# A decoder step on one core: tile 7's values ahead of two output parts, other places for identity matmuls and counts, V's sets in another order

## What is computed

```
z = rmsnorm(x, norm1_g) @ w_in            # rq rk rv rg mq mk mv
ret_o, state = retention_chunked(rq, rk, rv, state_ret)
moba_o = moba_attend_seq(mq, k_past + mk, v_past + mv)
mix = concat(groupnorm(ret_o) * ret_norm_g * silu(rg), moba_o)
h = x + mix @ w_out
n = rmsnorm(h, norm2_g)
logits = n @ router_w + router_b
top_v, top_i = top_k(logits, 4)
gates = softmax(top_v) spread over the experts top_i
for e in 32 experts:                      # 2048 gate/up columns, d_ff = 1024
    acc += gates[:, e] * (swiglu(n @ w_gate_up[e] + b_gate_up[e]) @ w_down[e] + b_down[e])
y = rmsnorm(h + acc, final_norm_g)
```

## Time and profile before

| what | value |
|---|---|
| time, median of 3 runs | 1268.71 us (1266.96 to 1270.87) |
| profiled execution, its own time | 1270.82 us |
| its span, first to last instruction | 1269.0 us |
| PE busy | 1207.8 us (95%) |
| DVE, ACT, POOL busy | 384.2, 232.7, 120.3 us |
| bytes moved | 500.64 MB, mean 395 GB/s |
| mean granted TensorE clock | 0.983 of full speed |
| chain that ended last | PE 61%, DMA 26%, DVE 7% |

### The profile page before, as it was taken

The page is one execution under the profiler, slowest core; times in us unless marked ns, Lnnn a source line. Parts: engine busy times, 40 slices in busy tenths (PEclk is TensorE's granted clock), DMA queues, the critical chain, the costliest instruction groups (busy, mean ns, idle before and its releaser), DMA issues.

```text
span 1269.0 us, 17410 instructions
## 1 busy us (share of the span) xinstructions
PE 1207.8 (95%) x7256; PEld 517.4 (41%) x7256; DVE 384.2 (30%) x552; ACT 232.7 (18%) x529; POOL 120.3 (9%) x117
## 2 busy tenths in 40 slices
PE   6999998699999999999999999999999999999997
PEld 3455445345534434343433434343434434343432
DVE  4999964153411211111122111111112211111113
ACT  3021153024201121110112112010102121111103
POOL 2222446641000000000000000000000000000000
PEclk8999999889899999999999999999999999999999
DMA  8999889968799999999999999999999999999994
GB/s 334 378 363 357 314 297 326 387 243 319 280 415 430 428 429 429 428 429 429 429 427 429 429 428 429 429 429 427 429 429 428 430 428 429 428 428 428 427 428 199
DMA packets 56604, 500.64 MB, mean 395 GB/s; under 512 B 6393, under 2 KB 6801, under 8 KB 27761
## 3 DMA queue, kind: packets, MB, share of 16 engines
q1 hardware_dynamic: 42128, 430.55, 81.1%
q0 software_dynamic: 14432, 69.47, 14.7%
HBM read 495.29 MB, written 4.72 MB: 394 GB/s over the span
## 4 chain that ended last, share of the span: by engine, by line
PE 61%; DMA 26%; DVE 7%; issue 4%; ACT 1%; SPq 0%; POOL 0%; DVEq 0%; POOLq 0%; ACTq 0%
PE psum L940 22%; DMA arena<-w_gate_up 21%; PE psum L971 12%; PE psum L852 6%; DVE arena L1430 5%; DMA arena<-w_down 3%; PE psum L858 2%; PE psum L502 2%; PE psum L697 2%; PE psum L870 2%; PE psum L589 2%; PE psum L882 2%; DMA arena<-cache_k,arena 1%; PE psum L889 1%; PE psum L428 1%
## 5 line engine op out<-in xcount | busy, mean ns | idle before, releaser
L940 PE MATMUL psum<-arena 128*64 128x512 f32 x1920 | 422.7, 594 | 15.7 <-DMA arena<-w_gate_up 15.6
L940 PEld LDWEIGHTS psum<-arena 128*64 128x64 f32 x1920 | 134.8, 137 | 300.1 <-issue 265.0
L1758 DVE TENSOR_SCALAR arena<-psum 128x512 f32<-128x512 f32 x32 | 22.1, 692 | 682.8 <-PE psum L940 643.5
L971 PE MATMUL psum<-arena 128*64 128x512 f32 x960 | 212.6, 595 | 0.0
L1096 ACT ACTIVATE arena<-psum 64x512 f32<-64x512 f32 (+3 forms) x184 | 93.5, 509 | 370.2 <-PE psum L971 170.7
L1430 DVE STREAM_TRANSPOSE arena<-arena 128x2048 f32<-128x2048 f32 x32 | 121.4, 3920 | 3.1 <-PE psum L488 1.9
L971 PEld LDWEIGHTS psum<-arena 128*64 128x64 f32 x960 | 66.4, 137 | 124.2 <-issue 122.4
L502 PE MATMUL psum<-arena 128*128 128x512 f32 x224 | 107.1, 617 | 0.5 <-ACT arena L1096 0.4
L1313 ACT ACTIVATE arena<-arena 128x512 f32<-128x512 f32 x30 | 18.9, 631 | 419.4 <-DVE arena L1758 419.4
L1096 ACT ACTIVATE arena<-psum,arena 128x128 f32<-128x128 f32 (+2 forms) x182 | 53.6, 397 | 171.2 <-PE psum L502 115.8
L852 PE MATMUL psum<-arena 128*128 128x128 f32 x512 | 80.1, 302 | 0.4 <-DVE arena L1679 0.4
(11 more groups left out here) (242 smaller groups left out, 724.3 us busy)
## 6 DMA issues: line engine op xcount, KB each, us to landing
arena<-w_gate_up SPq DMA_DIRECT2D x128, 2048.0 KB, 29.7
arena<-w_down SPq DMA_DIRECT2D x63, 2048.0 KB, 32.9
arena<-w_in SPq DMA_DIRECT2D x7, 2048.0 KB, 18.3
arena<-w_out SPq DMA_DIRECT2D x2, 2048.0 KB, 13.9
out<-arena SPq DMA_DIRECT2D x4, 512.0 KB, 3.0
out<-arena POOLq DMA_DIRECT2D x1, 2048.0 KB, 12.5
arena<-w_down SPq DMA_DIRECT2D x2, 1024.0 KB, 34.0
arena<-x_prompt SPq DMA_DIRECT2D x2, 512.0 KB, 5.6
```

What stands on the lines that cost most here:

```text
L940: last = mm(psum[64 * g:64 * (g + 1), b, :], xt[:, 2 * kk + m, lhs], gate_slot[slot][:, m, c:c + 512], start=False, stop=kk == 3 and m == ...
L971: last = mm(psum[64 * g:64 * (g + 1), 2, :], at_sb[:, m, SLOTS * q:SLOTS * (q + 1)], down_slot[slot][:, m, 512 * g:512 * (g + 1)], start=q ...
```

## The change

Eight edits, in the order of the diff. TensorE's `p_transposes(7)` and `values(7)` stand ahead of two output parts and of `sample_state(2)` and `(3)`, instead of behind them, and `evacuate_pt(7)` on ScalarE stands ahead of the sigmoid of the retention gate. `norm_transposes(1)` stands ahead of tile 0's logits, with two identity matmuls ahead of it; the identity matmul that stood ahead of tile 1's logits stands behind them; one more stands between the two groups of counts. The counts per pair stand behind the counts of ranks instead of behind the gather, and write bank 0 instead of bank 5. GpSimd's set 14 stands ahead of `v_block(1)`.

```
@@ tensor
             retention_output(0)
             retention_output(1)
+            pt = p_transposes(7)
+            values(7, pt)
             pe.wait_ge(own_ready, 1)
             output_part(1, 0, 5, attention)
             sample_state(2)
...
             output_part(0, 1, 6, attention)
             sample_state(3)
-            pt = p_transposes(7)
-            values(7, pt)
...
+            stay_awake(4, 2)
+            pe.wait_ge(hn_ready, 3)
+            norm_transposes(1)
             pe.wait_ge(a_empty, n_0[0])
             pe.wait_ge(d_empty, n_0[1])
             pe.wait_ge(router_in, 32)
             logits(0)
-            pe.wait_ge(hn_ready, 3)
-            norm_transposes(1)
             pe.wait_ge(a_empty, n_2)
             logits(2).then_inc(lg_full, 1)
-            stay_awake(7, 1)
             pe.wait_ge(a_empty, A.n)
             pe.wait_ge(d_empty, V.n)
             logits(1).then_inc(lg_full, 1)
+            stay_awake(7, 1)
...
             count(2, earlier, 2, start=False, stop=False)
+            stay_awake(7, 1)
             pe.wait_ge(picked_ready, 3)
             count(1, earlier, 1, start=False, stop=True)
             count(2, ones, 1, start=False, stop=True).then_inc(rank_full, 1)
+            for tile in range(TILES):
+                last = mm(psum[:, 0, 0:E], ones, picked[:, tile, :], start=tile == 0, stop=tile == TILES - 1)
+            last.then_inc(rank_full, 1)
...
             gather(0, 1)
-            for tile in range(TILES):
-                last = count(3, ones, tile, start=tile == 0, stop=tile == TILES - 1)
-            last.then_inc(rank_full, 1)
@@ scalar
             evacuate(ret_o[:, 1].rearrange("p h d -> p (h d)"))
+            evacuate_pt(7)
             wait_all(act, mark["z6"])
...
-            evacuate_pt(7)
@@ vector
-            tot = psum[:, 5, 3 * E:4 * E].rearrange("p (n e) -> p n e", e=2)
+            tot = psum[:, 0, 0:E].rearrange("p (n e) -> p n e", e=2)
@@ gpsimd
             v_set(13)
+            v_set(14)
             v_block(1)
-            v_set(14)
             v_set(15)
```

## The result

| | before | after |
|---|---|---|
| median, 20 runs each | 1268.12 us (1265.17 to 1272.44) | 1271.18 us (1266.64 to 1277.43) |
| ratio, 95% interval | | 1.0028 (1.0016 to 1.0041) |
| profiled execution, span | 1270.82, 1269.0 us | 1272.72, 1270.9 us |

The changed kernel takes 3.1 us more, by about the bound of 0.3%. I had forecast 1267.2, with 1270.9 as the upper end: the median lies 0.3 us above the range, and on the other side of no change.

A forecast was written before the change was run, and what follows sets the result against it. Bound by the expert-weight stream, so the loop start sets the end: +1.8 - 1.6 - 1.4 - 2.3 = -3.5 us on the profiled 1270.8 gives 1267.3, rounded with small change to 1267.2 us; range 1264.2 to 1270.9.

The forecast's parts named there:

- What bounds the kernel: Expert loop: bound by the weight stream; an earlier loop start moves the end one for one, until 6.6 us of pause are used.
- Part 1: Tile 7's transposes and `values(7)` ahead of two output parts: VectorE's states come later, costing +1.8 us on both paths.
- Part 2: Last V sets earlier: set 15 lands at 272.7 to 275.9, median 273.2, so no wait; far end costs 1.6 us.
- a landing after 274.3: Sign of being wrong: set 15 landing later than 274.3 us, when `values(7)` needs it halfway.
- Rival (b): GpSimd's `v_block(3)` multiply holds up VectorE's long product, +1.3 us on both paths: 1268.5 us; chance 0.20.
- part 3: Tile 1's transposes ahead of the logits, with identity matmuls: gather starts 1.6 us earlier (-2.1 + 0.35 + 0.1).
- Part 4: Pairs counted ahead of the gather: loop starts 2.45 us behind the gather instead of 3.9, a gain of 1.4 us.
- the gather's clock: Gather ahead of the loop: ran 10.4 us near 1.2 GHz, 6.4 at full clock; bounds 0 and -4.0, taken as -2.3 us.

The follow-up runs named there:

- e12: e7 with a buffer of its own for `v_block(3)`, so GpSimd makes it right behind `v_block(2)`; ratio 1.0009 to the kernel before.
- e7: Changed kernel with `load_turn(0)`, the 2 MB first expert load, held until set 14 has been used; ratio 1.0002 to the kernel before.
- e2: Kernel before with only tile 7's transposes and values moved ahead and set 14 ahead of `v_block(1)`, router part as before; 1274.78 us, ratio 1.0047.
- e4: Changed kernel with GpSimd's memset of y and `y_zero` ahead of the store of the states; 1273.75 us, ratio 1.0031 to the kernel before.
- e9: Changed kernel unaltered, run again as the control on the second chip; ratio 1.0018 to the kernel before.
- e10: e7 and e3 joined: first expert load held, and VectorE's states of head 2 behind the norm's last product; ratio 0.9992 to the kernel before.
- e1: Changed kernel with tile 7's transposes, values and ScalarE copy put back in their old places; 1265.84 us, ratio 0.9975 to the kernel before.
- e3: Changed kernel with VectorE's `new_states(2)` behind the last long product of the norm; 1269.79 us, ratio 0.9998 to the kernel before.
- e8: Kernel before with only GpSimd's set 14 moved ahead of `v_block(1)`; ratio 1.0017 to the kernel before.

## Where the prediction was right and where it failed

**What bounds the kernel** held. The span followed the start of the loop in every experiment, and the pause at the loop start took up most of the stream's later start: 5.0 of 6.6 us.

**Part 1, the order of the work: right.** I reckoned +1.8 us from moving `values(7)`; e12, in which TensorE doesn't wait for set 15 and VectorE's product isn't blocked, measured +1.72.

**Part 2: the step that failed.** "I take the median, 273.2, as most sets are at it: no wait." The set landed at about 276.2, beyond even the bound of 275.9, and the second half waited 3.51 us for it; the prediction had itself named a landing after 274.3 as a sign of being wrong. Two terms were too small, the landing and, further down, the issue.

The landing first. The row mixed sets of two kinds, and the trace of before could have told them apart. The same view of line 1904 there, first for the gathers issued from 240 to 258 us, then for the last four:

```profile
L1904 POOL DMA_INDIRECT arena<-cache_v,arena x9: 999/1003/1058, 240.3 to 258.0; - x9
...
DMA to landing us min/median/max: 8.3/8.4/9.3
```

```profile
L1904 POOL DMA_INDIRECT arena<-cache_v,arena x4: 1003/1003/1004, 263.3 to 267.2; - x4
...
DMA to landing us min/median/max: 11.0/11.1/11.5
```

The long landings were not a tail of all sets: they were all four of set 15, whose first gather was issued at 263.28, right behind `load_turn(0)`:

```profile
263.02 0.35 SPq L2008 DMA_DIRECT2D arena<-w_gate_up  x1
```

Before, no one waited for them. The question to ask of the set was whether its transfer shares the DMA, and the answer, 11.0 to 11.5 us behind 264.4, would have been a wait of 1.1 to 1.6 us as the likeliest case. e7 shows the cause.

The landing explains 2.9 of the 3.51 us (11.7 instead of 8.8). The issue explains more than the rest: I had the last gather 6.6 us ahead of the mark (271.01 - 264.4), and it was issued 4.93 us ahead of it (269.36 - 264.43), 1.7 us too late against a margin of 1.1. Even at the median landing TensorE would have waited 0.5 us. I had let set 15 start 2.6 us behind the start of `values(6)` (260.5 - 257.93). After, GpSimd's `v_block(1)` lay in between (the rows at 258.37 and 260.44), and it was 4.2 us; in e2 nothing but `values(6)` held the set, and it was 4.1 all the same (261.48 - 257.39). So the half of `values(6)` with the handing over to GpSimd took 1.5 us more than I gave it.

The bound was short for a third reason, because it priced the wait alone. Behind a wait of 3.51 us TensorE's clock was down, and the second half took 3.56 + 1.95 - 3.67 = 1.84 us more than before. Of all terms this was in none. It is no fixed price either: in e4 and e9 nothing was lost behind the wait.

**Rival (b) happened, and was priced right**: +1.3 us by my reckoning, 2.95 - 1.75 = 1.20 measured, and 1.20 in e12 against e7. All five profiled executions with the product behind that multiply show 2.95. I gave it 0.20 since the rows before showed only GpSimd paying. The rule of the Trainium skill that stood beside it ("SBUF — State Buffer", "Who interferes with whom": whoever of the two comes first blocks the other) agrees with every meeting here, those in which VectorE came second (2.95, 3.07 us) as well as those in which GpSimd did (2.54 in the earlier trace rows, 2.95 in e10).

The store's delay after the mark adds up: 1.72 (order) + 3.51 (wait) + 1.84 (clock) + 1.20 (product) = 8.27; measured 25.72 - 17.46 = 8.26. I had forecast the first term alone. On the other path, to the projection, VectorE's 8.26 met 1.0 us of slack (its product ended at 286.13 before, and the transposes began at 287.12), and the transposes behind the 1.96 us wait took 3.11 us to the output part instead of 1.89: 8.26 - 1.0 + 1.2 = 8.5, measured 26.55 - 18.00 = 8.55.

**Parts 3 and 4 and the gather: the sum was right, two terms of it were not.** From the end of the projection to the loop I reckoned -5.3 us; measured 25.13 - 30.32 = -5.2. But part 3 brought +0.1 instead of -1.6. The logits were done sooner (TensorE's counts, behind a wait of 0.93 us for VectorE, begin at 328.26, 11.01 us behind the projection, where before it was 322.67 - 310.11 = 12.56: -1.55 instead of -2.1), and then the new identity matmul and the one ahead of the gather, the latter in a stretch of clock 0.5, ate it: the one ahead of the gather took 2.06 us where I had put 0.9. Where the whole stretch ran at full clock, in e7, the whole part took 14.81 us, -1.2; where it was at the lower level from the counts on, 18.1 to 18.6 (e1, e3, e4, e9, e10, e12). Part 4 held: 2.35 us from gather to loop instead of 3.81, in every variant that has it (-1.46, reckoned -1.4). The gather took 6.70 instead of 10.51, -3.8 and not -2.3.

And most of that last gain can't be credited to the change. e2 and e8 have the router part of before, and their gathers took 7.61 and 7.73 us; the 10.51 of the profiled execution of before appeared in no other of the profiled ones. With the router part of after and all its identity matmuls it took 6.33 to 8.03. So the gather's clock varies between executions of either order, and I had counted -2.3 us as an effect: the means of the three profiles of the old order and the eight of the new one, 8.6 and 7.2 us, lie 1.4 apart, and 0.5 without the 10.51. By luck it did no harm to the forecast: I had started from a profiled execution 2.1 us above the median, and +1.8 - 1.6 - 1.4 = -1.2 on the median of 1268.7 gives 1267.5, next to my 1267.2.

**All together**, in the two profiled executions: +8.55 to the projection, +0.24 in it, -5.19 from its end to the loop, 3.60 us; the mark itself came 1.65 us earlier after (`sample_state(0)` ahead of it took 1.98 us instead of 3.78; with the same edit of GpSimd it took 3.78 in e2 and 1.98 in e3, so I take it for chance), so the loop started 1.95 us later. In medians, e2's +5.6 us and e1's -3.4 make +2.2, where the whole made +3.1. Is the store's extra delay all of the miss? Not quite: e12, where only the 1.72 us are left, came out at 1.0009 (0.9994 to 1.0024), and the forecast was 0.9988. In its profile the other part stands in the column ahead of the gather, 18.40 us where 14.4 were reckoned: identity matmuls and counts at the low clock. What the kernel before has there on this second chip is known only from e8, 16.20 us.

**What stays open.** The rest of the span behind the loop start was either near 928.4 or near 926.5 us, in a way that goes with no edit; no run here tells why. Why TensorE's clock was low in the counts of e1, and not in those of e7, isn't settled either.

## What to carry to other kernels

When a wait is moved ahead, ask of each transfer behind it what else is on the DMA at that moment, and split the landing times by that; a median over all of them is the price of none. And take the time from a release to the first transfer from a row, not from the matmuls' length. A block that is moved ahead of others on one engine delays every engine that was fed by those others, and may put two that had passed each other side by side: look at both queues at the new time. Identity matmuls on the path cost double where the clock is already low, and one execution's clock in one stretch is no property of the kernel: look for the same stretch in a second profile before crediting an edit with it.

## What was not expected of the hardware

- An indirect gather of 0.5 MB landed in 5.6 to 9.3 us with only its like beside it (the last sets before and after the change), and in 11.0 to 11.5 with one 2 MB direct load beside the set (9.8 to 11.7 after the change).
- A product of VectorE with two inputs in SBUF waited out a GpSimd multiply that had begun 0.56 us ahead, and the two can block each other in turn (2.95 and 3.07 us for 1.9 and 1.76).
- Two chips ran the same kernel at 1268 and 1296 us. The difference lies ahead of the loop, which starts at 342.38 us in the kernel after on one and at 373.96 on the other: from 170 to 290 us the kernel after moved 292 GB/s on one and 258 on the other, at granted clocks of 0.94 and 0.89.
